# Eleven page parts asked for in the latent prompt attention, later numbers read behind it; nine dilated value pieces loaded early, between the keys

## The reference

```python
def mla_attend(q_pos, q_lat, q_rope, ckv, krope, k_pos):
    s = jnp.einsum('bqhc,bkc->bhqk', q_lat, ckv) + jnp.einsum('bqhr,bkr->bhqk', q_rope, krope)
    s = s.astype(jnp.float32) * MLA_SCALE
    s = jnp.where((k_pos[None, :] <= q_pos[:, None])[None, None], s, -jnp.inf)
    p = jax.nn.softmax(s, axis=-1).astype(ckv.dtype)
    return jnp.einsum('bhqk,bkc->bqhc', p, ckv)
...
        mla_past = None if cache_mla is None else cache_mla[i][page_table].reshape(B, past_len, KV_LORA + D_ROPE)
...
    for g, (win, dil) in enumerate(SWA_GROUPS):        # (128, 1), (512, 4), (2048, 16)
        kv_new = qkv[:, :, 1:, g]
        ...
        kv_g = jnp.concatenate([prefix, kv_new], axis=1)
        new_bufs.append(kv_g[:, -win:])
        ...
        o, lse = map_query_blocks(
            lambda qp, qg: dilated_group_attend(qp, qg, kv_g, past_len - win, win, dil, bias), pos, qkv[:, :, 0, g])
```

## Time and profile before

| | |
|---|---|
| median of 3 runs | 2750.65 us (2747.92 to 2754.5) |
| the profiled execution | 2745.76 us, its span 2744.0 us |
| mean granted TensorE clock | 0.977 of full |
| latent prompt attention | 65 to 97 us |
| latent sample attention | 97 to 206 us |
| dilated prompt attention | 377 to 410 us |
| dilated sample attention | 410 to 546 us |

### The profile page before, as it was taken

How to read it: one execution, slowest core, us unless ns; L and a number is a source line. 1 busy time by engine, 2 the same in 40 slices (tenths; PEclk the granted TensorE clock), 3 DMA queues, 4 the chain that set the end, 5 groups by cost and what they waited for, 6 DMA issues and landing times. The chain is left out here.

```text
span 2744.0 us, 40512 instructions
## 1 busy us (share of the span) xinstructions
PE 2583.0 (94%) x16081; PEld 2151.7 (78%) x16081; DVE 1386.1 (51%) x3096; ACT 458.8 (17%) x1381; POOL 637.9 (23%) x619
## 2 busy tenths in 40 slices
PE   7889987898899999999999999989999999999997
PEld 5564463346499999999999866464999999999997
DVE  2430020122379979995553111223799799855541
ACT  3210120012111125420000010121211244300000
POOL 0005000000004425563331000000044255633310
PEclk9799998899999999999999999999999999999999
DMA  7789959996919989999998795948099899999994
GB/s 241 251 285 287 370 202 401 406 368 249 405 39 358 383 310 378 392 376 409 409 409 341 239 375 214 371 169 340 1 372 378 307 383 387 369 410 409 409 345 159
DMA packets 249129, 885.36 MB, mean 323 GB/s; under 512 B 27386, under 2 KB 34714, under 8 KB 238143
## 3 DMA queue, kind: packets, MB, share of 16 engines
q1 hardware_dynamic: 169374, 606.97, 59.3%
q0 software_dynamic: 79568, 275.81, 26.4%
HBM read 863.33 MB, written 109.08 MB: 354 GB/s over the span
## 5 line engine op out<-in xcount | busy, mean ns | idle before, releaser
L2929 PE MATMUL ps<-xT,front 128*128 128x192 f32 x4096 | 686.5, 327 | 6.6 <-DMA front<-in_peer_uT 6.5
L2929 PEld LDWEIGHTS ps<-xT,front 128*128 128x128 f32 x4096 | 663.2, 190 | 11.8 <-DMA front<-in_peer_uT 10.6
L2956 PE MATMUL ps<-p1e_S,p_qT 128*128 128x192 f32 x2048 | 336.6, 327 | 4.7 <-DMA p_qT<-in_peer_v 4.6
L2956 PE MATMUL ps<-p0e_S,p_qT 128*128 128x192 f32 x2048 | 336.3, 327 | 5.0 <-DMA p_qT<-in_peer_v 5.0
L2956 PEld LDWEIGHTS ps<-p0e_S,p_qT 128*128 128x128 f32 x2048 | 332.5, 190 | 8.6 <-DMA p_qT<-in_peer_v 8.5
L2956 PEld LDWEIGHTS ps<-p1e_S,p_qT 128*128 128x128 f32 x2048 | 332.5, 190 | 8.6 <-DMA p_qT<-in_peer_v 8.6
L2695 DVE CUSTOM_DVE_ANT_0 front<-front,x_tok 128x1024 f32<-128x1024 f32 x256 | 308.6, 1219 | 7.2 <-DMA front<-in_peer_u,p1e_expert 3.0
L2596 POOL DMA_INDIRECT front<-in_peer_u,p0e_expert x128 | 157.1, 1227 | 352.8 <-DVE p0e_dots L2695 171.6
L2596 POOL DMA_INDIRECT front<-in_peer_u,p1e_expert x128 | 157.0, 1226 | 350.3 <-DVE p1e_dots L2695 172.5
L2706 DVE SCALAR_TENSOR_TENSOR h_tok<-front,p1e_dots,h_tok 128x1024 f32<-128x1024 f32 x127 | 163.0, 1283 | 126.9 <-DMA front<-in_peer_v,p1e_expert 125.5
L2706 DVE SCALAR_TENSOR_TENSOR h_tok<-front,p0e_dots,h_tok 128x1024 f32<-128x1024 f32 x127 | 163.0, 1284 | 126.2 <-DMA front<-in_peer_v,p0e_expert 124.9
(11 more groups left out here) (474 smaller groups left out, 2905.4 us busy)
## 6 DMA issues: line engine op xcount, KB each, us to landing
front<-in_peer_uT SPq DMA_DIRECT2D x256, 512.0 KB, 7.0
p_qT<-in_peer_v SPq DMA_DIRECT2D x256, 512.0 KB, 7.3
out_swa_sample<-in_cache_swa_w SPq DMA_DIRECT2D x32, 2040.0 KB, 23.1
e_ring<-in_mla_pages SPq DMA_DIRECT2D x84, 272.0 KB, 4.6
e_ring<-in_swa_kT SPq DMA_DIRECT2D x16, 1024.0 KB, 9.6
e_arena<-in_swa_v SPq DMA_DIRECT2D x16, 1024.0 KB, 13.9
out_swa_sample<-in_cache_swa_w SPq DMA_DIRECT2D x8, 2016.0 KB, 30.1
e_ring<-in_attn_w_in SPq DMA_DIRECT2D x6, 2048.0 KB, 35.7
```

The source lines that it names most:

```text
L2929: mm = pe.matmul(k.ps[:, SB[i % len(SB)], 0:TD], ur[:, i % NU, c, :], k.xT[:, c, D0:T], start=(c == 0), stop=(c == KC - 1))
L2956: mm = pe.matmul(k.ps[:, c // 2, c % 2 * TD:(c % 2 + 1) * TD], vr[:, i % NV, c * P:(c + 1) * P], S[:, i, :], start=False, stop=(i == STEPS ...
```

## The change

In the latent part, `place_more` makes the last five slots at the start of `mla_prompt` and not of `mla_sample`. Beside `mla_prompt` SyncE now issues parts 4 to 10 (before 4 to 6), the seventh and later ones into the new slots, once the bias rows that stood in their place are stored. It reads no numbers ahead there. In `mla_sample` it issues three samples' new rows, part 11, and then reads the numbers of parts 12 to 19; later readings are eight parts ahead.

In the dilated part, the 48 stores of sample rows become three transfers from the scratch tensor to the outputs, between the prompt's key stores and value stores. Behind all stores, still in `swp`, nine value tiles of the samples 0 and 1 are loaded, those that lie over keys of `kv`, which nobody reads any more. In `sws` the rest of their values is asked for sample by sample behind `load_keys`: sample 0's behind no key load, sample 1's behind two. TensorE waits for the nine early tiles before the first values. In the expert stages the semaphore of three exponentials is merged with another, and the bank has 36.

```diff
-PARTS_EARLY, PARTS_LATER = (0, 1, 2, 3), (4, 5, 6)
-PARTS_NUMBERED_AHEAD = tuple(range(7, 16))
+PARTS_EARLY, PARTS_LATER = (0, 1, 2, 3), (4, 5, 6, 7)
+PARTS_MORE = (8, 9, 10)
+PARTS_NUMBERED_AHEAD = tuple(range(12, 20))
...
+VALUES_EARLY = ((0, 0, 3), (0, 6, 9), (0, 12, 13), (1, 0, 2))
...
                 for u in range(g * GB, (g + 1) * GB):
                     load_keys(u)
-                if g == 0 and a.get("before_values"):
-                    a["before_values"](sp)
-                for u in range(g * GB, (g + 1) * GB):
+                    if u < VS:
+                        load_values(u)
+                for u in range(max(g * GB, VS), (g + 1) * GB):
                     load_values(u)
...
+                if u == 0 and a.get("values_begun"):
+                    a["values_begun"](pe)
...
-    sp.dma_start(io["kv_new"], kv[0:64, 2, :]).then_inc(k.window_stored, 16)
-    n += 1
-    for g, (w, _) in enumerate(SWA_GROUPS):
-        for c in range(2):
+    sp.dma_start(io["kv_new"], kv[0:64, 2, :]).then_inc(k.new_stored, 16)
+    for c in range(2):
+        for g, (w, _) in enumerate(SWA_GROUPS):
...
-            for b in range(DEC_B):
-                dst_s = io[f"swa_sample{g}"][0, b, w - DEC_S:w, c].rearrange("w h d -> w (h d)")
-                sp.dma_start(dst_s, kv[8 * b:8 * b + 8, 2, cols]).then_inc(k.window_stored, 16)
+        if c == 0:
+            sp.wait_ge(k.new_stored, 16)
+            new = io["kv_new"].rearrange("(b s) (c g n) -> g b s c n", s=DEC_S, c=2, g=3)
+            for g, (w, _) in enumerate(SWA_GROUPS):
+                sp.dma_start(io[f"swa_sample{g}"][0, :, w - DEC_S:w].rearrange("b w c h d -> b w c (h d)"),
+                             new[g]).then_inc(k.window_stored, 16)
                 n += 1
...
+    def place_more(self, ctx):
+        more = self.k.sb(ctx, "ms_pages_more", [P, PAGE_PARTS - len(self.parts), 4, PAGE_ROW])
+        self.parts = self.parts + [more[:, i] for i in range(PAGE_PARTS - len(self.parts))]
+
     def load_later(self, sp):
         for n in PARTS_LATER:
+            if n == GATHERING:
+                sp.wait_ge(self.k.by_dist_stored, 16)
             self.load_part(sp, self.parts[n], self.k.pages_later, self.numbers(sp, n))
+        for n in PARTS_MORE:
+            self.load_part(sp, self.parts[n], self.k.pages_more, self.numbers(sp, n))
+
+    def number_ahead(self, sp):
         self.numbered = {n: self.numbers(sp, n) for n in PARTS_NUMBERED_AHEAD}
...
-            load_new(0)
-            for n in range(FIRST_PART, 4 * DEC_B):
+            for u in range(3):
+                load_new(u)
+            latent.load_part(sp, slot(PAGE_PARTS - 1), landed[PAGE_PARTS - 1], latent.numbers(sp, PAGE_PARTS - 1))
+            latent.number_ahead(sp)
+            for n in range(PAGE_PARTS, 4 * DEC_B):
                 wait(sp, v_used, n - PAGE_PARTS + 1)
...
+def preload_window_values(k, sp, room):
+
+    sp.wait_ge(k.window_stored, 16 * N_WINDOW_STORES)
+    for u, t0, t1 in VALUES_EARLY:
+        sp.dma_start(room["values"][:, u, t0:t1, :], k.io["swa_v"][u, :, t0:t1, :]).then_inc(k.values_early, 16)
...
+    tiles_left = {(0, 0): (3, 5), (0, 1): (5, 6), (0, 2): (9, 12), (1, 0): (2, 5)}
```

More of the change, by code:

```diff
@@ L60 @@
 SWA_CACHED = len(SWA_TILES) * P
-N_WINDOW_STORES = 1 + 2 * (1 + 2 + 2) + 2 * len(SWA_GROUPS) * DEC_B
+N_WINDOW_STORES = 2 * (1 + 2 + 2) + len(SWA_GROUPS)
 SWA_KEY_SLOTS = 4
+VALUES_EARLY = ((0, 0, 3), (0, 6, 9), (0, 12, 13), (1, 0, 2))
 SWA_KEYS = SWA_CACHED + 3 * DEC_S
@@ L92, in __init__ @@
         self.bias_tabled = ctx.enter_context(nc.semaphore("bias_tabled"))
+        self.new_stored = ctx.enter_context(nc.semaphore("new_stored"))
         self.window_stored = ctx.enter_context(nc.semaphore("window_stored"))
@@ L104, in __init__ @@
         self.pages_later = ctx.enter_context(nc.semaphore("pages_later"))
+        self.pages_more = ctx.enter_context(nc.semaphore("pages_more"))
         self.bias_landed = ctx.enter_context(nc.semaphore("bias_landed"))
@@ L108, in __init__ @@
         self.keys_landed = [ctx.enter_context(nc.semaphore(f"keys_landed{n}")) for n in range(SWA_KEY_SLOTS)]
+        self.values_early = ctx.enter_context(nc.semaphore("values_early"))
         self.mem_kv_stored = ctx.enter_context(nc.semaphore("mem_kv_stored"))
@@ L111, in __init__ @@
         (self.copies, self.zero_rows), self.n_copied = self.plan_copies(), 0
-        self.held, self.bank, self.blocks, self.bank_size = [], 0, 0, 37
+        self.held, self.bank, self.blocks, self.bank_size = [], 0, 0, 36
         names = [f"rows_landed{g}" for g in range(GATHERING)]
@@ L1668, in even_mixer @@
                     query_stage(k, e, weights, pages, bias)
+            with ExitStack() as cm:
+                pages.place_more(cm)
                 mla_prompt(k, e, pages, bias)
-            mla_sample(k, e, pages)
+                mla_sample(k, e, pages)
             mla_values_stage(k, e)
@@ L1919, in mla_sample @@
         mask = latent.mask
-        more = k.sb(ctx, "ms_pages_more", [P, PAGE_PARTS - GATHERING, 4, PAGE_ROW])
-        slots = latent.parts + [more[:, i] for i in range(PAGE_PARTS - GATHERING)]
+        slots = latent.parts
         pT = k.sb(ctx, "mls_pT", [P, 9, P])
@@ L1937, in mla_sample @@
         C, PG = 3, 3
-        FIRST_PART = len(PARTS_EARLY) + len(PARTS_LATER)
+        assert len(slots) == PAGE_PARTS
         def slot(n):
@@ L1973, in wait_part @@
                     pe.wait_ge(k.pages_later, 64 * len(PARTS_LATER))
+                elif n in PARTS_MORE:
+                    pe.wait_ge(k.pages_more, 64 * len(PARTS_MORE))
                 else:
-                    pe.wait_ge(landed[n % PAGE_PARTS], 64 * ((n - FIRST_PART) // PAGE_PARTS + 1))
+                    pe.wait_ge(landed[n % PAGE_PARTS], 64 * ((n - PAGE_PARTS + 1) // PAGE_PARTS + 1))
             def q(u, t):
@@ L2158, in swa_sample @@
     tiles_of = ((0, 5), (5, 9), (9, 13))
+    tiles_left = {(0, 0): (3, 5), (0, 1): (5, 6), (0, 2): (9, 12), (1, 0): (2, 5)}
     def load_values(sp, u, part, slot):
-        t0, t1 = tiles_of[part]
+        t0, t1 = tiles_left.get((u, part), tiles_of[part])
         yield sp.dma_start(vcache[:, slot, t0:t1, :], io["swa_v"][u, :, t0:t1, :])
@@ L2203, in swa_sample @@
         "ahead": ahead, "early": early, "first": lambda sp: early.load(sp, 1),
-        "before_values": lambda sp: sp.wait_ge(k.window_stored, 16 * N_WINDOW_STORES),
+        "before_values": None, "values_begun": lambda pe: pe.wait_ge(k.values_early, 16 * len(VALUES_EARLY)),
     })
@@ L2680, in gates @@
             def gates():
-                dve.wait_ge(exp_ready, 3)
+                dve.wait_ge(act_ready, 3)
                 for i, (_, n) in enumerate(TILES):
@@ L2741, in row @@
                 if n == HK:
-                    dve.wait_ge(act_ready, 1)
+                    dve.wait_ge(act_ready, 4)
                     link(dve.tensor_tensor(out=dots[:, :], in0=dots[:, :], in1=IJ[:, 0, 2, :], op=ALU.mult))
@@ L2835, in exponentials @@
                     act.wait_ge(diff_ready, i + 1)
-                    act.activation(best[0:n, i], best[0:n, i], ACT.Exp).then_inc(exp_ready, 1)
+                    act.activation(best[0:n, i], best[0:n, i], ACT.Exp).then_inc(act_ready, 1)
             def take_keys():
```

4 lines of the change are left out of this document (2 added, 2 removed).

## The result

The changed kernel takes 2763.57 us (median of 6 runs, 2758.81 to 2768.11), the kernel before 2750.52 us beside it (6 runs, 2747.92 to 2754.5). The ratio is 1.0047 with a 95% interval of 1.0037 to 1.0057, that is 13 us more (10 to 16). The forecast was 2760 with a range of 2751 to 2768, slower at 0.79. The profiled execution took 2758.81 us, its span is 2757.0, the mean granted clock 0.976.

A forecast was written before the change was run, and what follows sets the result against it. TensorE has matmuls in flight for 94% of the span; the dilated sample stretch is bound by transfers, the latent one's slow side is SyncE's issuing. Order +10.9, stores -0.8, latent 0 give +10.1: 2760 us, range 2751 to 2768.

The forecast's parts named there:

- The order, +10.9 us: Dilated sample stage: 17 value tiles ahead of the last key delay it at 0.64 us each, nothing recovers it; +10.9 us.
- The signs that the text named: Dilated sample stage: key waits about 11 us longer, last key near 452, sample 2's values issued at 465 to 467, DMA hole between.
- The stores, -0.8: End of dilated prompt attention: fewer store issues let the next stage start 0.8 us earlier, SyncE having some 10 us spare.
- Parts 7 to 10 early, 0 with bounds to +1: Latent prompt stage: SyncE's extra issues and readings take 14.0 us, done at about 91.8, hidden by 4.8 us; cost 0.
- Part 12 and the waits, 0: Latent sample stage: part 12 issued at 119 +- 0.5, two waits remain at 2 to 3 us each; gain 0.
- the reading behind part 23: Latent sample stage: one added page-number reading ahead of part 24, bounds 0 to +1.6 us, taken as 0.
- Only the amount counts: Rival, dilated sample stage: nine tiles fewer save 5.8 us whatever the order, time 2744; chance 0.08.
- The pages were the cause of the waits: Rival, latent sample stage: both waits and the slow matmuls behind them vanish, giving back 8.5 us, net +1.6, 2752; chance 0.08.
- A lower clock on top: Rival, dilated sample stage: longer key waits put twelve products behind the last key at 1.2 GHz; +16, 2766; chance 0.07.
- Half of it: Rival, dilated sample stage: the queue is looser and the last key moves by 5 us; +4, 2755; chance 0.05.
- The sum: Whole kernel: 10.9 - 0.8 + 0 = +10.1 us, giving 2760.8 on the median; likeliest's own range 2756 to 2766.

The follow-up runs named there:

- e7: Changed kernel without the early pieces: all 26 value tiles of samples 0 and 1 asked for between the keys; ratio to before 1.0072.
- e1: Changed kernel with all value loads of the dilated sample stage again behind all keys of their group; median 2754.03 us, ratio to before 1.0012.
- e3: Kernel before with only the latent part of the change (and the changed expert-stage semaphores); 2749.5 us, ratio to before 0.9997.
- e10: Kernel before plus merged stores and nine early tiles issued right behind the key stores; latent part and load order as before; ratio to before 1.0000.
- e11: Same kernel as e5, executed once more for a profile; 2763.37 us, dilated sample stage 150.1 us.
- e8: e10 with four key parts of the second group asked for ahead of sample 2's values; ratio to before 1.0001, dilated sample stage 141.9 us.
- e2: Kernel before with the dilated part of the change alone, latent part as before; 2763.61 us, ratio to before 1.0047.
- e4: Changed kernel with page numbers read nine parts ahead, not eight, and no reading behind part 23; ratio to before 1.0040.
- e9: e10 with two key parts of the second group asked for ahead of sample 2's values; median 2747.97 us, ratio to before 0.9993.
- e5: Changed kernel with early tiles issued right behind the key stores, and the wait for other stores moved ahead of sample 0's values; ratio to before 1.0046.

## Why the prediction was right, and where it was off

**The order, +10.9 us: right in mechanism, too small.** The stage grew by 13.6 us. The count was right: per tile 0.64 us in e7, and 0.66 to 0.72 with early tiles in the queue, so 17 tiles cost 10.9 to 12.2. With no tile ahead of a key (e1), the stage is still 2.1 us longer than before, and 11.5 + 2.1 is the 13.6. The prediction had nothing for those 2.1 us; it took the early tiles to be out of the way when the stage begins (below). Its sentence that this stretch is bound by its transfers "all of the time" was not so at its start either, where the share is 0.04. The signs that the text named came: the wait for keys +11.4 us (11 forecast), the hole at a share of 0.01 ("well under a half"), 13.8 us from the last key to sample 2's issue (471.33 - 457.56 = 13.77). The last key at 457.56 and the issue at 471.33 are later than the 452 and 465 to 467 of the text by more than the 2.6 us by which the stage starts later; the missing part is 2.4 us in both.

**The stores, -0.8: right in size, wrong in a sentence.** The dilated prompt stage took 413.13 - 381.45 = 31.7 us against 410.50 - 377.78 = 32.7: -1.0. (The thirteen issues of the text are fourteen: 1 + 5 + 3 + 5.) It is 33.2 in e3, which has the old stores, and 31.6 to 31.9 in every other run. But "Even with a wait for the stores to land, SyncE has some 10 us to spare" was wrong: SyncE's last issue ends at 412.20, the stage's last copy at 412.81, so 0.6 us were to spare. The text priced the issues and not the landing, and the store of the new rows took 17.2 us to land. That is the step that failed. It let the early tiles go out only at 410.22, and most of their transfer stood ahead of the keys. That the 2.1 us are this transfer is shown in part: e10, where the tiles go out at 401.81, 11 us ahead of the stage, has a stage 1.6 us shorter than e1; e11 gave 0.6 only, with its own wait in the way. Whether all of the 2.1 us would come back stays open.

**Parts 7 to 10 early, 0 with bounds to +1: right.** SyncE's sixteen issues and four readings ran from 77.54, the end of part 6's, to 96.65. That is 19.1 us and not 14.0, past the 91.8 us of the text. The last four of them:

```profile
94.21 2.44 SPq L1929 DMA_DIRECT2D ms_pages_more<-in_mla_pages  x4
```

The stage's last work in this kernel ends on ScalarE at 96.55 + 0.28 = 96.83, so 0.2 us of the 4.8 were left; the stage took 97.59 - 66.44 = 31.15 us, and 97.24 - 66.10 = 31.14 before. The lower DMA share in 97:119 (0.36 for 0.81) shows the early parts at work and nothing gained by it.

**Part 12 and the waits, 0: right in sum.** Part 12 was issued at 119.80 (119 +- 0.5 forecast). The sign of two waits of 2 to 3 us each did not come: there were three, of 3.77, 1.12 and 2.36. Over all profiles the latent sample stage differs by 0.4 us within a spread of 3 and more; the reading behind part 23, bounded by +1.6, can't be seen.

**The rivals.** *Only the amount counts* is out by e10 and e1: with the order of before, nine tiles fewer in the stage gave nothing. My own theory of the filled hole, which rested on the same thought, fell with e8. *The pages were the cause of the waits* is out by e3. *A lower clock on top* did not come in its place: the twelve products behind the last key ran at 2.84 us for six, as before. But the clock was 0.76 in 413:455, against 0.95 in 410:442, and in two other executions that cost something. In the changed kernel the transfers were still the later side there: the DMA share is 0.97 or more in every window of 1 to 4 us up to 455, and TensorE waited 0.23 us for the last key. In e2 and e4, which have the same dilated part, it did not wait for it at all and took it 45.1 and 45.2 us after the start, in place of 44.4. In e2 the clock was at its lower level for 6 us behind the wait for the seventh key part, and the DMA engines had run dry ahead of 461.02, where TensorE takes the last key:

```profile
446.00:452.00 6.00, 5.00 (x46) 1.62 (x50) 0.00 (x0) 0.00 (x0) 0.00 (x0) 0.50 1.02 421
459.00:461.00 2.00, 2.00 (x11) 0.42 (x10) 0.69 (x1) 0.00 (x0) 0.00 (x0) 1.00 0.03 12
```

So the rival has a small share of its own, at most the 0.3 to 0.8 us by which the stages of e4 and e2 are longer. *Half of it* is out: the last key moved by 44.4 - 31.1 = 13.3 us.

**The sum.** 13.6 - 1.0 + 0.4 = 13.0 us, and the medians differ by 13.05, closer than the interval of 10 to 16 us lets one expect. The forecast of +10.1 was 2.9 us low and 13.0 lies above its own +8 to +12; the measured 2763.57 is inside 2756 to 2766 only by the 3 us that this range had for scatter. The two profiled executions differ by 16.2 us at the end of this stage and by 13.0 at the end of the span. The 3 us come back in two stages of the second layer, whose work is the same: at a granted clock of 0.97 for 0.94, and 1.00 for 0.89. In e2 they do not come back, so they are the clock's, not the change's. For e1 to e11 the sums of the stages fall within their intervals. Two are at the edge: e7 with 17.1 - 1.0 + 0.4 = 16.5, where the ratio says 16 to 23, and e8 with 4.7 - 1.0 = 3.7, where it says -3 to +4.

Open stays whether e9 is faster than before: its stages say 1.9 us, its ratio 0.9993 with an interval of 0.9982 to 1.0004. It is faster than the changed kernel by some 15 us. Not tried was a third value slot or a fifth key slot, which by e8 is what could turn fewer tiles into time.

## What to carry to other kernels

A queue that reads 1.0 busy is not yet a budget from which every byte saved comes back. Find the place where the slots are full and the next load waits for a computation, and count the bytes behind what that computation needs: those fill a hole that exists anyway, and moving them ahead costs their full transfer time, here 0.64 to 0.72 us for each 256 KB. Price the landing of stores and not only their issue, when something waits for them. And take the spread of a stage over several kernels that share it before a wait in one trace is given a cause.

## What the runs showed of the hardware

- The same 1104 matmuls of the latent sample stage took 108.2 to 113.1 us in eleven profiles, with two to five waits ahead of page products, at different samples from run to run. The share of the DMA engines was 0.99 in 162:190 before and 1.00 in the changed kernel. No run shows what decides which part comes late.
- A store of 768 KB of new rows, issued at 381.52 behind four key parts and two weight loads, took 5.30 us to issue and 17.2 us to land.
- With the same order of loads, the granted clock between waits for keys differed from one execution to the next: 0.62 in 445:449 of the changed kernel, 0.50 in 446:452 of e2, at much the same place behind the seventh key part.
- One execution of 7 of the kernel e5 took 6432 us; the other six took 2757 to 2767. Its granted clock is recorded as 1.0, yet TensorE is busy for 6343.6 us (2582.7 in the changed kernel) and VectorE for 1396.7 (1386.3). No run explains it.
